# Opening of a 256-token, two-layer block: x^T from the host and two weight blocks in float32

## What is computed

```python
def rms_norm(x, g, eps=NORM_EPS):
    xf = x.astype(jnp.float32)
    y = xf * lax.rsqrt(jnp.mean(xf * xf, axis=-1, keepdims=True) + eps)
    return (y * g.astype(jnp.float32)).astype(x.dtype)

def swiglu(x, wg, wu, wd):
    return (jax.nn.silu(x @ wg) * (x @ wu)) @ wd

x = x + 0.5 * swiglu(rms_norm(x, ffn1_norm[l]), ffn1_wg[l], ffn1_wu[l], ffn1_wd[l])
```

## Time and profile before

| what | value |
|---|---|
| median of 3 runs | 857.02 us (856.53 to 857.32) |
| the profiled execution's own time | 857.04 us |
| span of the profiled execution | 855.2 us |
| PE busy | 846.6 us, 99% of the span |
| DVE busy | 637.6 us, 75% |
| ACT busy | 525.0 us, 61% |
| granted TensorE clock | digit 9 (90% or more) in all 40 slices |

### The profile page before, as it was taken

How to read it: one execution, slowest core, us unless ns; L and a number is a source line. 1 busy time by engine, 2 the same in 40 slices (tenths; PEclk the granted TensorE clock), 3 DMA queues, 4 the chain that set the end, 5 groups by cost and what they waited for, 6 DMA issues and landing times.

```text
span 855.2 us, 11976 instructions
## 1 busy us (share of the span) xinstructions
PE 846.6 (99%) x4775; PEld 736.6 (86%) x4775; DVE 637.6 (75%) x788; ACT 525.0 (61%) x738; POOL 59.5 (7%) x65
## 2 busy tenths in 40 slices
PE   9999999999999999999999999999999999999997
PEld 8988888888889998888888887888888898888885
DVE  5999999987698656765466468758777677877873
ACT  6677777766574544653554456548666665576772
POOL 0022322210000000000000000100000001000001
PEclk9999999999999999999999999999999999999999
DMA  8976566655544655576456545586666655853501
GB/s 275 348 244 201 174 196 198 196 160 159 201 148 144 202 194 176 172 253 234 152 166 231 194 148 191 193 282 226 203 198 195 211 177 169 264 178 108 189 1 50
DMA packets 123991, 162.47 MB, mean 190 GB/s; under 512 B 3864, under 2 KB 111136, under 8 KB 123808
## 3 DMA queue, kind: packets, MB, share of 16 engines
q1 hardware_dynamic: 122320, 154.89, 54.9%
q0 software_dynamic: 1312, 6.29, 2.2%
q10 hardware_dynamic: 304, 0.53, 0.2%
HBM read 160.65 MB, written 1.05 MB: 189 GB/s over the span
## 4 chain that ended last, share of the span: by engine, by line
PE 98%; DVE 1%; ACT 0%; POOL 0%; issue 0%; POOLq 0%; DVEq 0%
PE pAcc L456 23%; PE pG L390 9%; PE pU L390 9%; PE pAcc L390 7%; PE pG L396 5%; PE pR L390 5%; PE pU L396 5%; PE pM L390 4%; PE pAcc L396 3%; PE pR L396 2%; PE pAcc L434 2%; PE pAcc L435 2%; PE pM L396 2%; PE pAcc L436 2%; PE pG L517 1%; PE pM L436 1%
## 5 line engine op out<-in xcount | busy, mean ns | idle before, releaser
L326 DVE TENSOR_TENSOR lo<-raw,hi 128x2048 fp32r<-128x2048 f32 x131 | 298.5, 2288 | 52.9 <-ACT hi L321 52.8
L321 ACT ACTIVATE hi<-raw 128x2048 fp32r<-128x2048 f32 x140 | 265.5, 1906 | 19.6 <-PE pAcc L436 5.6
L390 PE MATMUL pG<-xT,hi 128*128 128x512 f32 x336 | 83.4, 390 | 0.0
L390 PE MATMUL pU<-xT,hi 128*128 128x512 f32 x320 | 80.0, 392 | 0.0
L456 PE MATMUL pAcc<-hi,h_hi 128*128 128x512 f32 x240 | 74.5, 392 | 0.0
L390 PEld LDWEIGHTS pG<-xT,hi 128*128 128x128 f32 x336 | 62.8, 188 | 13.6 <-issue 0.7
L456 PE MATMUL pAcc<-lo,h_hi 128*128 128x512 f32 x240 | 74.0, 389 | 0.0
L456 PE MATMUL pAcc<-hi,h_lo 128*128 128x512 f32 x240 | 73.9, 389 | 0.0
L1118 ACT ACTIVATE h_hi<-h 128x512 fp32r<-128x512 f32 x28 | 17.7, 633 | 80.6 <-PE pAcc L456 74.8
L390 PEld LDWEIGHTS pU<-xT,hi 128*128 128x128 f32 x320 | 58.0, 189 | 10.7
L1637 DVE TENSOR_TENSOR h_lo<-h,h_hi 128x512 fp32r<-128x512 f32 x28 | 19.3, 688 | 46.1 <-ACT h_hi L1118 46.1
(11 more groups left out here) (505 smaller groups left out, 1633.9 us busy)
## 6 DMA issues: line engine op xcount, KB each, us to landing
raw<-in_a_w_in SPq DMA_DIRECT2D x24, 1024.0 KB, 5.3
raw<-in_ffn_wd SPq DMA_DIRECT2D x22, 1024.0 KB, 5.8
raw<-in_ffn_wg SPq DMA_DIRECT2D x21, 1024.0 KB, 5.4
raw<-in_ffn_wu SPq DMA_DIRECT2D x21, 1024.0 KB, 6.6
raw<-in_w_in SPq DMA_DIRECT2D x16, 1024.0 KB, 5.5
raw<-in_a_w_out SPq DMA_DIRECT2D x8, 1024.0 KB, 5.0
raw<-in_w_kv SPq DMA_DIRECT2D x8, 1024.0 KB, 5.3
raw<-in_b_w_qz SPq DMA_DIRECT2D x8, 1024.0 KB, 5.7
```

Source lines behind the costliest of these rows:

```text
L321: act.activation(HI[n % NHL][:, :], RAW[n % NRAW][:, :], ACT.Copy).then_inc(S["hi"], 1)
L326: dve.tensor_tensor(LO[n % NHL][:, :], RAW[n % NRAW][:, :], HI[n % NHL][:, :].bitcast(f32), ALU.subtract).then_inc(S["lo"], 1)
L390: end = pe.matmul(v3(bank[:, :], 2), wh[:, k, w], x4[:, :, k, :], start=start and k == 0, stop=not start and k == KD - 1, skip_group_check ...
```

## The change

x is also laid out by the host as x^T (`x_t`, 128 feature rows, by tile, chunk and token), and loaded in that form to a new buffer `XRAW`, which shares its place with `XN`; the eight transposes of each tile are gone. x itself, needed for the residual, is loaded later by SP as one DMA of 1 MB, between blocks 7 and 8. The norm's sum of squares now runs over partitions: ACT squares x^T with a strided write (`square_first`), DVE sums over the chunks (`sum_first`), and PE sums over partitions by a product with a column of 1/D (`mean_square`). The gain's load goes ahead of the second quarter of x^T on ACT's queue. Block 1 is multiplied in float32 for tile 1 too and no longer split; block 2 is split in halves instead. Block 4's load waits for block 0 alone, block 5's for block 1. The bias inputs come ready and repeated over partitions from the host, in two DMAs behind block 3. `xt_ps` counts four less afterwards, and h of tile 1 in the first iteration is scaled by 1/rms (before, only tile 0's).

```diff
+        XRAW = at("x_t", NT * D, f32, cursor[0] - 4 * NT * D)
...
+        XSQ, SSQ, MEAN = X, SB, ST[:, 110:111]
...
+        VAR = (ACC[1][:, 0:1], ACC[2][:, 0:1])
...
-            if n >= NRAW:
+            if n in (NRAW, NRAW + 1):
+                sp.wait_ge(S["used"], n - NRAW + 1)
+            elif n > NRAW:
                 sp.wait_ge(S["lo"], n - NRAW + 1)
...
-        def hi_half(act, half):
-            act.wait_ge(*((full[1], LANDED[1]) if half else (S["first1"], 16)))
+        def hi_first(act, half):
+            if not half:
+                act.wait_ge(full[UNSPLIT], LANDED[UNSPLIT])
             c = slice(half * KD * BC // 2, (half + 1) * KD * BC // 2)
-            op = act.activation(HI[1][:, c], RAW[1][:, c], ACT.Copy)
+            op = act.activation(HI[UNSPLIT][:, c], RAW[UNSPLIT][:, c], ACT.Copy)
+            op.then_inc(*((S["hi"], UNSPLIT + 1) if half else (S["hi_first"], 1)))
+
+        def lo_first(dve, half):
+            dve.wait_ge(*((S["hi"], UNSPLIT + 1) if half else (S["hi_first"], 1)))
+            c = slice(half * KD * BC // 2, (half + 1) * KD * BC // 2)
+            op = dve.tensor_tensor(LO[UNSPLIT][:, c], RAW[UNSPLIT][:, c], HI[UNSPLIT][:, c].bitcast(f32), ALU.subtract)
             if half:
-                op.then_inc(S["hi"], 2)
-            else:
-                op.then_inc(S["hi_first"], 1)
-
-        def lo_of_half(dve, half):
-            dve.wait_ge(*((S["hi"], 2) if half else (S["hi_first"], 1)))
-            c = slice(half * KD * BC // 2, (half + 1) * KD * BC // 2)
-            op = dve.tensor_tensor(LO[1][:, c], RAW[1][:, c], HI[1][:, c].bitcast(f32), ALU.subtract)
-            if half:
-                op.then_inc(S["lo"], 2)
+                op.then_inc(S["lo"], UNSPLIT + 1)
...
-        def load_x(engine, t, c):
-            engine.dma_start(X[:, t * D + c * 512:t * D + (c + 1) * 512],
-                             T["x"][0, t * P:(t + 1) * P, c * 512:(c + 1) * 512]).then_inc(S[f"x_in{t}{c}"], 16)
+        def load_x_t(engine, b):
+
+            c = slice(b * 512, (b + 1) * 512)
+            engine.dma_start(XRAW[:, c], T["x_t"][:, c]).then_inc(S[f"x_in{b}"], 16)
 
         def load_gain_first(engine):
 
             engine.dma_start(G8, T[GAINS[0]][0].rearrange("(k p) -> k p", p=P)).then_inc(S["gain0"], 16)
+
+        def load_x(sp):
+
+            sp.wait_ge(S["x_sum"], 2)
+            sp.dma_start(v3(X[:, :], NT), T["x"][0].rearrange("(t p) c -> p t c", p=P)).then_inc(S["x_rows"], 16)
...
-        def x_transposes(pe, t, half):
-            b = 2 * t + half
-            pe.wait_ge(S[f"x_in{t}{half}"], 16)
-            for k in range(4):
-                c = t * D + (4 * half + k) * P
-                end = pe.transpose(XBANK[b][:, k * P:(k + 1) * P], X[:, c:c + P], IDENT[:, :])
-            end.then_inc(S["xt_ps"], 1)
...
+        def mean_square(pe, t):
+
+            pe.wait_ge(S["x_sum"], t + 1)
+            pe.matmul(VAR[t], SSQ[:, t * P:(t + 1) * P], MEAN, start=True, stop=True).then_inc(S["x_var"], 1)
+
         def pe_start(pe):
 
-            busy(pe, 7)
-            x_transposes(pe, 0, 0)
+            busy(pe, 5)
             pe.wait_ge(S["gain0"], 16)
             pe.transpose(ACC[1][:, 0:KD], G8, IDENT[0:KD, 0:KD]).then_inc(S["gc_ps"], 1)
-            x_transposes(pe, 0, 1)
+            busy(pe, 4)
             pe.wait_ge(S["xf0"], 1)
             pe.wait_ge(S["first0"], 16)
             first_block(pe, 0, G, 0, range(0, 4))
             pe.wait_ge(S["xf1"], 1)
             pe.wait_ge(full[0], LANDED[0])
-            first_block(pe, 0, G, 0, range(4, 6))
+            first_block(pe, 0, G, 0, range(4, KD))
+            mean_square(pe, 0)
+            pe.wait_ge(S["xf2"], 1)
+            first_block(pe, 0, G, 1, range(0, 4))
             power_row(pe, 0)
-            first_block(pe, 0, G, 0, range(6, KD))
-            x_transposes(pe, 1, 0)
-            x_transposes(pe, 1, 1)
+            pe.wait_ge(S["xf3"], 1)
+            first_block(pe, 0, G, 1, range(4, 6))
+            mean_square(pe, 1)
+            first_block(pe, 0, G, 1, range(6, KD)).then_inc(S["used"], 1)
             pe.wait_ge(S["first1"], 16)
-            first_block(pe, 1, U, 0, range(0, 4))
+            first_block(pe, 1, U, 0, range(0, 2))
             power_row(pe, 1)
+            first_block(pe, 1, U, 0, range(2, 4))
             pe.wait_ge(full[1], LANDED[1])
             first_block(pe, 1, U, 0, range(4, KD))
-            pe.wait_ge(S["xf2"], 1)
-            pe.wait_ge(S["xf3"], 1)
-            first_block(pe, 0, G, 1, range(0, KD)).then_inc(S["used"], 1)
-            pe.wait_ge(S["lo"], 2)
-            pe.wait_ge(S["xt_lo"], 3)
-            to_tokens(pe, 1, U, XT, (1,), half_way=4).then_inc(S["used"], 1)
+            first_block(pe, 1, U, 1, range(0, KD)).then_inc(S["used"], 1)
+            pe.wait_ge(S["xt_lo"], 4)
...
         def xt_first(dve, b):
-            dve.wait_ge(S["xt_ps"], b + 1)
-            dve.tensor_tensor(xf(b), v3(XBANK[b][:, :], 4), fbc(GC[:, 4 * (b % 2):4 * (b % 2) + 4], P),
+            dve.wait_ge(S[f"x_in{b}"], 16)
+            dve.tensor_tensor(xf(b), x_raw(b), fbc(GC[:, 4 * (b % 2):4 * (b % 2) + 4], P),
                               ALU.mult).then_inc(S[f"xf{b}"], 1)
+
+        def squares(t):
+            return XSQ[:, t * D:(t + 1) * D].rearrange("p (c k) -> p c k", k=KD)
+
+        def square_first(act, b):
+            act.wait_ge(S[f"x_in{b}"], 16)
+            half = slice(4 * (b % 2), 4 * (b % 2) + 4)
+            act.activation(squares(b // 2).rearrange("p c k -> p k c")[:, half, :], x_raw(b), ACT.Square).then_inc(S["ssq"], 1)
+
+        def sum_first(dve, t):
+            dve.wait_ge(S["ssq"], 2 * t + 2)
+            dve.tensor_reduce(SSQ[:, t * P:(t + 1) * P], squares(t), AX.X, ALU.add).then_inc(S["x_sum"], 1)
+
+        def variance_first(dve, t):
+            dve.wait_ge(S["x_var"], t + 1)
+            c = RS_COL["norm", 0, t][0]
+            dve.tensor_scalar(ST[:, c:c + 1], VAR[t], 1e-6, None, ALU.add).then_inc(S["var"], 1)
...
+            if r == 0:
+                dve.wait_ge(S["x_rows"], 16)
...
-                        dve.tensor_tensor(H[:, BC:512], U[:, BC:512], SA[:, BC:512], ALU.mult).then_inc(S["h"], 1)
+                        k = RS_COL["norm", 0, 1][0]
+                        dve.scalar_tensor_tensor(out=H[:, BC:512], in0=U[:, BC:512], scalar=ST[:, k:k + 1], in1=SA[:, BC:512],
+                                                 op0=ALU.mult, op1=ALU.mult).then_inc(S["h"], 1)
...
-            load_x(sp, 0, 0)
+            load_x_t(sp, 0)
             load_half(sp, 0, 0)
             load_half(sp, 0, 1)
-            load_x(sp, 1, 0)
-            load_x(sp, 1, 1)
+            load_x_t(sp, 2)
+            load_x_t(sp, 3)
             load_half(sp, 1, 0)
             load_half(sp, 1, 1)
             load_block(sp, 2)
-            sp.dma_start(POS[:, 0:TOK], T["positions"][0].partition_broadcast(P),
-                         allow_slow_non_contiguous=True).then_inc(S["bias_pos"], 16)
-            sp.dma_start(POS[:, 3 * TOK:3 * TOK + NT], T["positions"][0].rearrange("(t p) -> p t", p=P),
-                         allow_slow_non_contiguous=True).then_inc(S["bias_pos"], 16)
-            sp.dma_start(RBI[:, :], T["rel_bias"].rearrange("b h -> (b h)").partition_broadcast(P),
-                         allow_slow_non_contiguous=True).then_inc(S["bias_pos"], 16)
-            sp.dma_start(STAB[:, 4 * NSTEP:5 * NSTEP], T["steps"].partition_broadcast(P),
-                         allow_slow_non_contiguous=True).then_inc(S["bias_pos"], 16)
             load_block(sp, 3)
+            sp.dma_start(POS[:, 0:TOK + NT], T["bias_positions"]).then_inc(S["bias_pos"], 16)
+            sp.dma_start(TABLES[:, 4 * NSTEP:], T["bias_tables"]).then_inc(S["bias_pos"], 16)
             for n in range(LEAD + 1, NB):
                 b = BLOCKS[n - LEAD]
-                if b == ("ffn1", "gate", 3):
+                if b == ("ffn1", "gate", 2):
+                    load_x(sp)
+                elif b == ("ffn1", "gate", 3):
...
+            pool.memset(MEAN, 1.0 / D).then_inc(S["mean"], 1)
...
-            load_x(act, 0, 1)
             load_gain_first(act)
+            load_x_t(act, 1)
             act.wait_ge(S["half"], 1)
             warm(act, ACT.Square)
-            for t in range(NT):
-                for c in range(2):
-                    act.wait_ge(S[f"x_in{t}{c}"], 16)
-                    square(act, 0, t, c)
+            for b in range(4):
+                square_first(act, b)
+            warm(act, ACT.Silu)
             xt_hi_first(act, 0)
             xt_hi_first(act, 1)
-            hi_half(act, 0)
-            hi_half(act, 1)
-            warm(act, ACT.Silu)
             xt_hi_first(act, 2)
             xt_hi_first(act, 3)
-            hi(act, 2)
+            hi_first(act, 0)
+            hi_first(act, 1)
...
-            variance(dve, 0, 0)
+            sum_first(dve, 0)
+            xt_first(dve, 2)
+            xt_first(dve, 3)
```

(63 more changed lines are left out.)

## The result

The changed kernel takes 858.19 us (median of 14 runs), the kernel before 857.09 in as many: ratio 1.0016, 95% interval 1.0009 to 1.0023. The forecast was 856.8 and no difference that can be told. The time lies in the range (855.8 to 858.5), but it moved up, clear of its interval, by 1.1 us.

What follows compares the result with a forecast made beforehand. PE was taken to bound the kernel, through its arrival at block 2. From the profiled 857.04 us, -0.16 for PE's work and -0.1 for the landing gave 856.8, no difference that can be told; range 855.8 to 858.5.

Steps and rivals of the forecast that it cites:

- Where to look: Whole kernel: PE bounds it, busy 99% of the span, so what counts is when PE reaches block 2, before at 21.42.
- the pivot at 8.39: Block 0, tile 0: its second half's landing sets PE's restart at 8.39, if four matmuls (1.73 us) are done by then.
- rival (a): Opening: PE's clock stays at half rate into block 0, costing +1.1 to +1.8 us, or 1.7 more; chance 0.20.
- The break that I named: PE's warm-up: the changed order has a break of 0.4 to 0.8 us in the middle, counted for a slow clock.
- The promised 0.16: PE's work up to block 2: 3.91 us removed, 3.75 added, so PE arrives 0.16 earlier, at 21.26.
- The landing: Block 0's half block in the opening: lands earlier by between nothing and 0.35 us, taken as 0.1.
- Float32 against three parts: Block 1, tile 1: float32 product takes 3.45 us by the trace, against 2.87 in three parts; the four-pass rule gives 3.83.
- Strided squares: ACT's squares of x^T: if strided writes doubled their 0.63 us, PE might wait 0.4 at the second `mean_square`.
- Cover: Inputs from other engines and loads are ready before PE asks, costing nothing; smallest margin 0.55 us, at block 2.
- (c): Block 2: its preparation is late and PE waits, +0.3 us if 1 us longer, +1.8 if 2.5; chance 0.08.
- (d): Later loads: block 5 or 8 comes late behind x, costing up to 2 us, 859; chance 0.03.
- (b): Opening: the start is the real bound, so an earlier start and landing win 1.0 us, 856.0; chance 0.12.

Runs made afterwards that it cites:

- e12: Changed kernel with the second piece of x^T loaded ahead of the gain, warm-up matmuls still five and four; median 858.64 us.
- e9: Changed kernel with the second piece of x^T ahead of the gain and warm-up matmuls seven and two instead of five and four; median 856.91 us.
- e1: Changed kernel with its nine warm-up matmuls in one piece ahead of the gain's transpose, instead of five and four around it; median 859.41 us.
- e8: Kernel before with nine warm-up matmuls instead of seven; median 857.47 us.
- e7: Changed kernel with the second piece of x^T ahead of the gain and six instead of four warm-up matmuls behind the gain's transpose; median 858.50 us.
- e2: Changed kernel with six instead of four warm-up matmuls behind the gain's transpose; median 857.65 us.
- e5: Changed kernel with seven instead of five warm-up matmuls ahead of the gain's transpose, four still behind it; median 857.41 us.
- e3: Kernel before with five instead of seven warm-up matmuls; median 857.76 us.
- e11: Kernel before with five instead of seven warm-up matmuls, run once more for another profile; median 858.49 us.
- e6: Kernel before with the gain loaded ahead of the second piece of x on ACT's queue; median 857.31 us.
- e10: Kernel before with no warm-up matmuls instead of seven; median 857.89 us.
- e4_again: Changed kernel unchanged, run once for a second profile; 857.59 us.

## Why the prediction went wrong, point by point

- **Where to look** was right: PE's arrival at block 2 is the whole effect, and the difference of arrivals gives that of the times to 0.1 us.
- **The failed step** is "the pivot at 8.39 holds". The step gave block 0's start as 6.0 to 6.7 and took its four matmuls at 0.43. The start was 6.73, but they ran at 0.86. This is rival (a), as it was described: it had a chance of 0.20 and happened in half of the runs. Its prices, +1.1 to +1.8 with 1.7 more if all eight are slow, fit the upper group (+1.6 to +3.5 over 857.09). In the profile the first five matmuls were slow. I had counted "most of the time is still filled" against it. The break that I named does count (e12 against e9), and e1 against e8 points at the idle time right ahead of block 0 too, which I had passed over. The lower group, at 857.45 in its median, wasn't at the forecast either: in its profile the first records were slow too, and block 0 began at 6.66.
- **`mean_square`** was put at 0.15 each. It takes 0.12, and the group behind it 0.10 more (1.83 for what takes 1.73): 0.22, my upper end. From the end of tile 0's block to block 2 it is 23.56 - 12.53 = 11.03; before it was 21.42 - 10.50, and 0.11 for the `power_row` inside block 0: 11.03 too. The promised 0.16 is not there. What the transposes and the wait give (1.04), the float32 product (0.58) and two narrow products (0.44) take.
- **The landing** was put at 0.1 earlier. The first half took up to 1 us longer (5.3 to 5.9 instead of 4.8) with the gain first; the second landed at 8.0 to 8.9 (before, 8.3). The reason given, that SP's queue has more to itself, was wrong in this order.
- **The gain** was expected between 4.35 and 4.75. PE transposed it at 3.95, so it landed within 3.2 us of its start, not 3.6 to 4.0. Second in the queue, in e7, it took 3.3.
- **Float32 against three parts**: 0.43 a matmul stood; the four passes of the Trainium skill, "FP8 and Floating Point Precision", section TensorE Precision Notes, would by my estimate have been 3.83 a block and tile; 28 records in 6.05 are 3.46.
- **Strided squares**: 1.14 instead of 0.63, nearly the doubling that I had tried. That agrees with the rule in "SBUF — State Buffer" of the Trainium skill, section Door 1; no run has the same squares with a contiguous write. PE did not wait for them.
- **Cover**: the branch from `power_row(1)` to the lo part of block 2 was worked out as 5.5 us. It took 22.84 - 17.51 = 5.3, and ended 0.7 ahead of PE. Rivals (c) and (d) did not come. (b), the start as the bound, is half right: e9, whose block 0 began at 6.06 in PE's timeline against 6.65 in e2 and 7.21 in e5, is 0.3 to 0.6 better than these, each taken against the kernel before beside it, not 1.0.

Still open: what decides when TensorE's clock rises. In the profiles it rose as early as 4.75 us and as late as 11.0, and at three moments with the same work of PE. Of runs over 858.1 there were 0 of 111, 0 of 11 and 0 of 11 in the kernel before, e8 and e9, and 1 of 11 each in e2 and e5; against 7 of 14 in the changed kernel, 5 of 6 in e1, 7 of 11 in e12, and 11 of 19 in e3 and e11 together. Two pairs with the same number of warm-up matmuls point at PE's idle time in the first 7 us: e9 and e12, and e8, where transposes fill it, and e1. But e6 (4 of 11, no idle time in its profile) and e10 (5 of 11 with no warm-up) don't fit a rule by number of matmuls or by idle time.

## What to carry to other kernels

Read the rate of an opening off the distance of equal matmuls, not off the printed clock or its mean, and time it in ten runs or more: an edit of the first 6 us can widen the spread where the median of three shows nothing. An edit that takes work away from PE ahead of its first real matmul may have to be given warm-up work in its place, without idle time in it and ending by the landing, not behind it. Here moving two matmuls ahead of a wait (e9 against e12) cured as many runs as adding two (e2 against the changed kernel), and cost no later start. Work taken off PE (here sixteen transposes) is only a gain net of what is put in, narrow products at their full 0.22 us included.

## What was not expected of the hardware

- The issue of a small load held SP for 3.33 us (`bias_positions`, one row a partition) where the broadcast before had held it for 4.1, and block 3, now ahead of it, for 3.08. Preparing the data on the host did not make the issue short. The long issue that begins between 5.1 and 6.4 us falls on whichever load stands there: 3.1 to 4.7 on block 3 in the changed kernel and its variants, 3.3 to 4.5 on `positions` in the kernel before and its variants. That a full queue is the reason is not shown. The 3.3 of `bias_positions`, some 3 to 5 us later, comes on top.
- One run-to-run spread goes with the order of two loads on another engine's queue (e6: 4 of 11 over 858.1, kernel before: none), with PE's own program unchanged. What changes for PE is when the second piece of x is there, 5.79 instead of 4.53.
- With no warm-up and PE idle until 4.18, the clock still rose at 7.63 us in the profiled run, earlier than with five and four matmuls in e4_again (7.91).
- At the end of the changed kernel's trace the granted clock reads 0.50 from 854.1 us on, when PE has nothing left to do; this, and not the opening, is what the printed mean of 0.998 shows.
